# A top-2 expert encoder: the up projection's matmuls made for 32 places instead of 64

## The reference, cut to what matters

```python
for e in range(N_EXPERTS):                       # 16 experts
    h = jax.nn.silu(t @ w1[e]) * (t @ w3[e])     # up projection: 1024 -> 512, twice
    y = y + combine[:, e:e + 1] * (h @ w2[e])    # down projection: 512 -> 1024
```

## Time and profile before

| | |
|---|---|
| median of 3 runs | 647.18 us (646.18 to 647.7) |
| the profiled execution | 647.33 us |
| its span, first to last instruction | 645.5 us |
| PE busy | 630.8 us (98%), 2953 matmul records |
| PE weight loads busy | 278.7 us (43%), 2953 records |
| DVE, ACT, POOL busy | 209.7, 179.5, 53.6 us |
| DMA | 229.61 MB, mean 356 GB/s |

### The profile page before, as it was taken

How to read it: one execution, slowest core, us unless ns; L and a number is a source line. 1 busy time by engine, 2 the same in 40 slices (tenths; PEclk the granted TensorE clock), 3 DMA queues, 4 the chain that set the end, 5 groups by cost and what they waited for, 6 DMA issues and landing times.

```text
span 645.5 us, 7957 instructions
## 1 busy us (share of the span) xinstructions
PE 630.8 (98%) x2953; PEld 278.7 (43%) x2953; DVE 209.7 (32%) x633; ACT 179.5 (28%) x440; POOL 53.6 (8%) x61
## 2 busy tenths in 40 slices
PE   8999999999999999999999999999999999999995
PEld 5445545633433533533344455474343343343331
DVE  1665833511302302311233767243221221212112
ACT  2136641211202202111231677221202202212112
POOL 0015420000000000000010475000000000000000
PEclk9999999999999999999999999999999999999999
DMA  8999909499999999999999996585999999999992
GB/s 319 284 270 420 366 5 387 162 426 422 421 421 418 372 424 422 422 423 422 401 297 247 411 402 198 225 356 213 424 420 422 417 423 374 423 422 422 421 422 80
DMA packets 43203, 229.61 MB, mean 356 GB/s; under 512 B 8272, under 2 KB 8562, under 8 KB 18595
## 3 DMA queue, kind: packets, MB, share of 16 engines
q1 hardware_dynamic: 41532, 224.66, 88.8%
q0 software_dynamic: 1312, 4.23, 2.0%
q10 hardware_dynamic: 326, 0.31, 0.2%
HBM read 228.10 MB, written 1.08 MB: 355 GB/s over the span
## 4 chain that ended last, share of the span: by engine, by line
PE 92%; ACT 3%; DVE 3%; issue 1%; DMA 1%; POOL 0%; DVEq 0%; ACTq 0%
PE ps L1387 34%; PE ps L1415 18%; PE ps L1154 12%; PE ps L1241 8%; PE ps L1348 5%; PE ps L1364 5%; PE ps L1223 2%; PE ps L1189 2%; PE ps L1210 2%; PE ps L1397 1%; ACT attw L541 1%; PE ps L1308 1%; DMA ring<-in_ln_mix_dram 1%; PE ps L1102 1%; PE ps L1174 0%
## 5 line engine op out<-in xcount | busy, mean ns | idle before, releaser
L1387 PE MATMUL ps<-ring,work 128*64 128x512 f32 x512 | 111.3, 593 | 0.0
L1387 PE MATMUL ps<-attw,work 128*64 128x512 f32 x512 | 111.2, 592 | 0.0
L1154 PE MATMUL ps<-attw,work 128*128 128x512 f32 x192 | 87.4, 598 | 0.1
L1415 PE MATMUL ps<-ring,work 128*64 128x512 f32 x384 | 85.9, 594 | 0.8
L967 DVE COPY work<-ps 32x512 f32<-32x512 f32 x64 | 43.7, 683 | 104.4 <-PE ps L1415 104.0
L955 DVE TENSOR_TENSOR work<-work,ps 128x256 f32<-128x256 f32 x32 | 12.0, 418 | 185.9 <-PE ps L1387 185.9
L1387 PEld LDWEIGHTS ps<-attw,work 128*64 128x64 f32 x512 | 36.8, 137 | 73.1 <-issue 73.1
L1387 PEld LDWEIGHTS ps<-ring,work 128*64 128x64 f32 x512 | 36.6, 137 | 72.2 <-issue 72.0
L617 ACT COPY work<-ps 32x512 f32<-32x512 f32 x64 | 36.9, 577 | 106.6 <-PE ps L1415 106.3
L1241 PE MATMUL ps<-attw,work 128*128 128x512 f32 x128 | 59.6, 601 | 0.7 <-issue 0.5
L1154 PEld LDWEIGHTS ps<-attw,work 128*128 128x128 f32 x192 | 34.6, 190 | 37.9 <-issue 37.4
(11 more groups left out here) (151 smaller groups left out, 489.8 us busy)
## 6 DMA issues: line engine op xcount, KB each, us to landing
ring<-in_w_dram SPq DMA_DIRECT2D x112, 1024.0 KB, 16.4
attw<-in_w_dram SPq DMA_DIRECT2D x80, 1024.0 KB, 16.9
attw<-in_w_qkv_dram SPq DMA_DIRECT2D x4, 2048.0 KB, 19.3
attw<-in_w_o_dram SPq DMA_DIRECT2D x8, 1024.0 KB, 23.1
attw<-in_w_qkv_dram SPq DMA_DIRECT2D x8, 512.0 KB, 12.1
ring<-bias_rows POOLq DMA_DIRECT2D x16, 256.0 KB, 7.1
x_sb<-in_x_dram SPq DMA_DIRECT2D x2, 512.0 KB, 6.8
out_dram<-x_sb SPq DMA_DIRECT2D x2, 512.0 KB, 4.5
```

The lines of the kernel that those rows point to most:

```text
L1154: last = pe.matmul(ps[:, g, :], xT[:, k, P * tt:P * tt + P], wqkv[part][:, k, :], start=(k == 0), stop=(k == KB - 1))
L1387: last = pe.matmul(ps[64 * e:64 * e + 64, 6 + which, :], xg[:, k, c:c + 2 * SLOTS], w13(which, k // 4)[:, e, k % 4, :], start=(k == 0), st ...
L1415: last = pe.matmul(ps[64 * e:64 * e + 64, half, :], hT[:, k, 64 * e:64 * e + 64], w2(kh)[:, e, k % 2, 512 * half:512 * half + 512], start= ...
```

## The change

In the up projection each matmul call of an expert's 64 columns becomes two calls of 32 columns, one for each token tile. Four calls a block `k` write partitions 0, 32, 64 and 96 and up, with the array's columns in four groups of 32. The two calls of one expert stream the same 512 columns of weights. Results, buffers, waits and semaphores are the same; `last` is now the fourth call.

```diff
@@ -1382,11 +1382,11 @@
                                 pe.wait_ge(m.xg_copied, QUARTERS * G + k // 2 + 1)
                             elif not j and not which and k == 0:
                                 pe.wait_ge(m.xg_copied, QUARTERS * G + QUARTERS)
-                            for e in range(2):
-                                c = 2 * SLOTS * (2 * j + e)
-                                last = pe.matmul(ps[64 * e:64 * e + 64, 6 + which, :],
-                                                 xg[:, k, c:c + 2 * SLOTS], w13(which, k // 4)[:, e, k % 4, :],
-                                                 start=(k == 0), stop=(k == KB - 1), tile_position=(0, 64 * e))
+                            for row in range(0, P, SLOTS):
+                                c = 4 * SLOTS * j + row
+                                last = pe.matmul(ps[row:row + SLOTS, 6 + which, :], xg[:, k, c:c + SLOTS],
+                                                 w13(which, k // 4)[:, row // (2 * SLOTS), k % 4, :],
+                                                 start=(k == 0), stop=(k == KB - 1), tile_position=(0, row))
                             if k % 4 == 3:
                                 last.then_inc(m.w13_used, 1)
```

## The result

The changed kernel takes 649.11 us as a median of five runs (648.75 to 649.19), the kernel before 646.9 (645.99 to 647.7): 1.0034 times as long, with a 95% interval of 1.002 to 1.0049. It is slower, by 2.2 us. The profiled execution took 649.19 us, its span is 647.4.

A forecast was written before the change was run, and what follows sets the result against it. PE was taken to bound the expert stage; up's rounds added nothing, 14 shape changes added 1.9 us, bringing the span from 645.5 to 647.4 and the forecast median to 649.1 us, 0.3% slower, range 646.9 to 656.

The forecast's parts named there:

- seams: Tile shape changes from down to up: next load not drawn ahead, 0.135 us with a later fourth group, 14 places, 1.9 us.
- The asymmetry: In the expert stage, time added on PE lengthens the kernel; time taken from PE could end in waits for weights.
- Calls and rounds: Up's calls go from 512 to 1024, PE's records from 2953 to 3977; still 32 rounds a pair, nothing added.
- The lower of the two bounds: In up, a round (one record per column group) stays at 0.429 us with four records; the upper bound added 220 us.
- Issue: Issuing four records with their loads, 8 instructions per round in up: taken as no cost, at most 8 us.
- Weight loads: Up's loads of 32 columns instead of 64 lie beside the round before: cost nothing, gain nothing.
- Rival D: Up's rounds paced by the weight load, so narrower loads save up to 46 ns each: 626 us, faster; chance 0.03.
- Rival A: No seam between down and up when only column width changes: 647.2 to 647.4 us, no change; chance 0.13.
- Rival B: Up's four groups don't run fully side by side: 869 us in full, or anything from 651 upwards; chance 0.16.
- Rival C: Longer loop code refetched at 4 jumps back, shown by over some 22 instruction packets: 653 to 657 us; chance 0.06.
- Nothing is late next: DVE and ACT are waited for little and SP's buffers come free 1.9 us later by the end: no added time.
- the free start: In up, a record starts when its column group is free, whatever stands ahead of it; no time added.

The follow-up runs named there:

- e1: Changed kernel with the down projection also split into four column groups of 32; 648.46 us, 1.0026 times the kernel before.
- e6: Kernel before with one of eight blocks left out of every up, all weights still loaded; 644.92 us, 0.998 times the kernel before.
- e10: Kernel before with four of eight blocks left out of up in each layer's last pair only, all weights still loaded; 648.01 us, 1.0025 times.
- e2: Kernel before with only down split into four column groups of 32, up left at 64; 649.17 us, 1.0033 times.
- e3: Changed kernel with half of up's blocks put back to 64 columns, so the width changes three times more in each pair; 655.52 us, 1.0133 times.

## Why the prediction was right

*The bound.* Among the experts the chain ran through PE alone, and 14 seams of 0.14 us on it appeared in full. (The prediction read PE's waits as having none on a DMA. There is one of 0.5 us, at the kernel's start, before any expert.) The asymmetry that the prediction asked to keep in mind turned out sharper than it said: e1, e6 and e10 show that weights and PE end almost together in each layer. Time put on PE shows; time taken from it does not. In the changed kernel the chain itself goes through a DMA at the end of the second layer, 18.25 us for the last weights.

*Calls and rounds.* 3977 records as counted, and a round of four takes 0.43 us. The lower of the two bounds was right, from the row that it was taken from, the second stream that cost nothing. e1_both32 shows it without any seam: 13.73 us.

*Issue.* Eight loads within 0.16 us at the start of an up: taken as nothing, rightly.

*Weight loads.* They became shorter (110 ns instead of 137) and this changed nothing, as they lie beside the stream. Rival D is out; by e6 and e10 the weights couldn't have followed a faster PE either.

*The seam.* 0.10 and 0.02 to 0.03 us in the timeline, as estimated; with the later end 0.135 was foretold and 0.14 measured. e2 and e3 confirm it from the other side (0.97 and 0.48 us, so the wider first load costs more, as the prediction's line says) and at 62 places. Rival A is out: a change between two column widths alone, with all 128 rows, has the full seam.

*Rival B.* No part of it: no round is longer. Its rule from the Trainium skill (TensorE: Matmul & The Clock Gate, Part 3, "What overlaps and what doesn't"), matmuls in strict program order, doesn't hold in these runs: with blocks of four calls the second expert starts while three earlier records of the first wait. Nor did the 2.38 for three groups carry over that the Trainium skill gives (same page, "Measured speedup vs the span model"); four groups run side by side here in full, 13.73 us in e1_both32 as in two groups.

*Rival C.* 21 instruction packets instead of 18, under the 22 that the prediction set as its sign; the code is longer, and PE's list has no wait that is new but the one for weights.

*The other engines.* "Nothing is late next" was wrong by 0.7 us: the last weights of each layer had about 0.2 us to spare, and with the change they come too late. The prediction's DMA row said that the engines are full; it didn't follow how late the last weights land.

*The number.* The mechanism and its size are right, but the fit to 0.01 us in the median (649.1 and 649.11) is luck, and so is that of the span (647.4 both times). The late weights added 0.7 us that the prediction hadn't, and the profiled execution gained 0.45 at its start by chance; the median of the kernel before, with more runs, came out 0.3 under the one that the forecast was built on.

*What it had not seen.* That the free start has a limit of three waiting records for each group. Two records a call, one call for each group in turn, stay within it, so the assumption held for this change, though not in general. My expectation for e1 failed by 1.5 us, since I took the seam for the only thing between that kernel and the one before. That its weights come too late for PE is shown, but not why. In the first layer they land at 314.8 and 314.9 us in the profiled executions of before and of e1, and PE wants them 1.2 us sooner in e1, 1.1 of which it was ahead from the start. In the second they land at 632.0 us instead of 630.7, although they were asked for 0.5 us sooner, at the same DMA rate; the cause of that is open.

## What to carry to other kernels

Splitting a matmul's stationary columns finer gained nothing here, where all 128 columns were in use already: the moving stream sets the round. Count instead how often the shape of the tile changes along the queue, at 0.10 us plus the load that is no longer hidden (0.02 for 32 columns, 0.05 for 64, 0.10 for 128), and keep neighbouring stages in one shape. Before paying for a faster engine, take some of its work away and see whether the time follows. And look at when the last weights land: with 0.2 us to spare, 1 us more or less on PE already moves a wait.

## What the runs showed of the hardware

- Four column groups of 32 run side by side in float32 with no loss: 13.73 us for 128 records of 512 columns, as for 64 records in two groups.
- Records pass others of another column group that stand ahead of them, as long as no more than three records of a group wait. With 8 and 16 records of a group in a row up took 15.84 and 22.48 us instead of 13.73; with 4 in a row 13.79.
- A change of tile shape keeps the next weight load from being drawn ahead: 0.96 us between loads instead of 0.43, from 128x64 to 64x128 tiles (up into scatter) and also when only the width changes, from 64 to 32 columns (0.96) or from 32 to 64 (0.97).
- A wait can cost more than itself: with 15.8 us of waits in six places, the same down records took 8.8 us longer, at a granted clock of 0.65 in one stretch of 7 us.
